# A sixth Strassen pair in the feed-forward blocks of a two-layer trunk

## The reference, cut to what matters

```python
def swiglu(h, w_in, w_out):
    g, u = jnp.split(h @ w_in, 2, axis=-1)
    return (jax.nn.silu(g) * u) @ w_out

for layer in range(DEPTH):          # DEPTH = 2
    ...                             # mixer
    x = x + swiglu(rms_norm(x, ffn_norm[layer]), w_ffn_in[layer], w_ffn_out[layer])
```

## Time and profile before

| | us |
|---|---|
| median of 3 runs | 2021.05 |
| lowest, highest | 2020.53, 2021.08 |
| the profiled execution's own time | 2020.83 |
| its span, first to last instruction | 2019.0 |
| TensorE busy | 2007.1 |
| VectorE busy | 1649.1 |
| ScalarE busy | 1179.2 |

### The profile page before, as it was taken

The page is one execution under the profiler, slowest core; times in us unless marked ns, Lnnn a source line. Parts: engine busy times, 40 slices in busy tenths (PEclk is TensorE's granted clock), DMA queues, the critical chain, the costliest instruction groups (busy, mean ns, idle before and its releaser), DMA issues.

```text
span 2019.0 us, 24662 instructions
## 1 busy us (share of the span) xinstructions
PE 2007.1 (99%) x9266; PEld 1664.0 (82%) x9266; DVE 1649.1 (82%) x1560; ACT 1179.2 (58%) x1195; POOL 170.6 (8%) x216
## 2 busy tenths in 40 slices
PE   9999999999999999999999999999999999999998
PEld 7888888888888888888888887888888888888886
DVE  5666776779999999999987477779999999999995
ACT  6745645555565555665557466565656556655554
POOL 0000000100111110111100000100111101111010
PEclk9999999999999999999999999999999999999999
DMA  8755444857998888998877643766988889888885
GB/s 275 236 188 167 155 150 139 273 195 232 263 270 250 251 242 256 270 260 246 243 236 230 198 138 138 235 223 229 261 256 256 238 254 266 259 259 242 243 261 160
DMA packets 237188, 461.40 MB, mean 229 GB/s; under 512 B 16481, under 2 KB 21377, under 8 KB 236993
## 3 DMA queue, kind: packets, MB, share of 16 engines
q1 hardware_dynamic: 202832, 386.97, 57.0%
q0 software_dynamic: 30496, 69.22, 16.8%
q10 hardware_dynamic: 3792, 4.34, 0.7%
HBM read 401.10 MB, written 17.29 MB: 207 GB/s over the span
## 4 chain that ended last, share of the span: by engine, by line
PE 92%; DVE 5%; ACT 1%; DMA 1%; issue 1%; ACTq 0%; SPq 0%; DVEq 0%
PE ps L1753 58%; PE ps L1538 29%; DVE g_lo L1279 1%; PE ps L1644 1%; DVE w_lo L918 1%; DVE w_lo L1284 1%; DMA raw<-in_w_ab_in 1%; DVE w_sum L1267 0%; PE ps L1564 0%; PE ps L1904 0%; PE ps L1879 0%; ACT junk L509 0%; ACT w_hi L466 0%; PE ps L1892 0%; DMA x<-in_x 0%
## 5 line engine op out<-in xcount | busy, mean ns | idle before, releaser
L1279 DVE TENSOR_TENSOR g_lo<-g_raw,g_hi 128x2048 fp32r<-128x2048 f32 x240 | 547.2, 2287 | 55.6 <-ACT g_hi L718 32.5
L918 DVE TENSOR_TENSOR w_lo<-raw,w_hi 128x1024 fp32r<-128x1024 f32 x248 | 294.6, 1220 | 151.5 <-ACT w_hi L466 144.9
L718 ACT CAST g_hi<-g_raw 128x2048 fp32r<-128x2048 f32 x140 | 265.6, 1912 | 157.7 <-PE ps L1753 151.5
L466 ACT ACTIVATE w_hi<-raw 128x1024 fp32r<-128x1024 f32 x248 | 253.9, 1056 | 144.1 <-DMA raw<-in_w_ab_in 55.4
L711 ACT CAST g_hi<-g_raw 128x2048 fp32r<-128x2048 f32 x100 | 191.5, 1915 | 215.9 <-DVE g_raw L1261 215.9
L1753 PE MATMUL ps<-g_hi,xT_hi 128*128 128x512 f32 x780 | 303.6, 389 | 0.9 <-DVE w_lo L1284 0.8
L1753 PE MATMUL ps<-g_hi,xT_lo 128*128 128x512 f32 x780 | 303.4, 389 | 0.0
L1538 PE MATMUL ps<-w_hi,xT_hi 128*128 128x512 f32 x672 | 264.4, 393 | 0.6 <-DVE w_lo L918 0.6
L1753 PE MATMUL ps<-g_lo,xT_hi 128*128 128x512 f32 x680 | 264.5, 389 | 0.0
L1538 PE MATMUL ps<-w_hi,xT_lo 128*128 128x512 f32 x672 | 261.8, 390 | 0.0
L1538 PE MATMUL ps<-w_lo,xT_hi 128*128 128x512 f32 x672 | 261.6, 389 | 0.0
(11 more groups left out here) (226 smaller groups left out, 3039.8 us busy)
## 6 DMA issues: line engine op xcount, KB each, us to landing
g_raw<-in_w_ffn_in SPq DMA_DIRECT2D x320, 512.0 KB, 4.8
g_raw<-in_w_ffn_out SPq DMA_DIRECT2D x160, 512.0 KB, 4.7
raw<-in_w_ab_in SPq DMA_DIRECT2D x96, 512.0 KB, 4.8
x<-y POOLq DMA_DIRECT2D x80, 512.0 KB, 6.8
raw<-in_w_qkv SPq DMA_DIRECT2D x40, 512.0 KB, 4.6
raw<-in_w_ab_out SPq DMA_DIRECT2D x32, 512.0 KB, 4.9
raw<-in_w_ffn_in SPq DMA_DIRECT2D x32, 512.0 KB, 4.7
raw<-in_w_c_out SPq DMA_DIRECT2D x32, 512.0 KB, 4.7
```

Of the source, the lines that this page charges most:

```text
L466: act.activation(w_hi[:, s, :], raw[:, s % RAWS, :], ACT.Copy).then_inc(hi_ready, 1)
L718: act.copy(dst[:, 0:4, :].rearrange("p s w -> p (s w)"), src[:, :, :].rearrange("p s w -> p (s w)")).then_inc(group_hi_ready, 1)
L918: dve.tensor_tensor(w_lo[:, s, :], raw[:, s % RAWS, :], w_hi[:, s, :], ALU.subtract).then_inc(lo_ready, 1)
L1279: ins = dve.tensor_tensor(lo_part[:, 0:4, :].rearrange("p s w -> p (s w)"), src[:, :, :].rearrange("p s w -> p (s w)"), hi_part[:, 0:4, :] ...
```

## The change

One of the three plain groups becomes a Strassen group: pair 5 now is the sixth "strassen" pair, and the order is S S S P S S S P. The rest of the edits follow from it. The hi places of groups 0 and 3 change roles (`HI_OF`), since group 0 now needs seven tiles. The token sums hold 6 pairs; two of the four `s_lo` move to the place of constants that are no longer read. Inside a Strassen group the three products of x and s_sum 3 that share banks P2, P4, P3 come first, then the four others. In group 0 TensorE waits ahead of P1 and P6 for the third y copy and ahead of P7 and P5 for the fourth; in block 1 it waits at these places for silu and `hidden` of block 0. ScalarE's program has copy 0, hi(0), copy 1, hi(1), copy 2, then the first part of hi(2), copy 3, and the second part of hi(2). Before it was hi(0), copies 0 and 1, hi(1), copy 2, hi(2), copy 3. The two parts of a Strassen hi are the four tiles of the pair and the three sums.

```diff
-GROUPS_UP = [("plain", 5), ("strassen", 0), ("strassen", 1), ("strassen", 2),
-             ("plain", 6), ("strassen", 3), ("strassen", 4), ("plain", 7)]
+GROUPS_UP = [("strassen", 0), ("strassen", 1), ("strassen", 2), ("plain", 6),
+             ("strassen", 3), ("strassen", 4), ("strassen", 5), ("plain", 7)]
+HI_OF = [3, 1, 2, 0]
...
+        s_lo_at = [bias_at + 52 * KB, bias_at + 55 * KB, consts_at + 512, consts_at + 512 + s_size]
...
             def hi_group(f, layer, g, first, base, between=None):
...
                     act.copy(dst[:, 0:4, :].rearrange("p s w -> p (s w)"),
                              src[:, :, :].rearrange("p s w -> p (s w)")).then_inc(group_hi_ready, 1)
+                    if between is not None:
+                        between()
                     act.wait_ge(sum_step, f * (3 * PAIRS) + (layer * BLOCKS * 3 * PAIRS + n + 3))
...
+                    if not first:
+                        copy_y(before, layer, 0)
                     hi_(0)
                     if not first:
-                        copy_y(before, layer, 0)
                         copy_y(before, layer, 1)
                     hi_(1)
                     if not first:
                         copy_y(before, layer, 2)
-                    hi_(2)
-                    if not first:
-                        copy_y(before, layer, 3)
+                    hi_group(f, layer, 2, first, base, None if first else lambda: copy_y(before, layer, 3))
                     hi_(3)
...
-                                      first and q < 2, last and q >= 2)
+                                      first and q == 1 and t == 1, last and q >= 2)
...
-                for bank, a, slot, alone in ((P1, x_part(2 * p, t0), 0, True), (P6, s_part(1), 4, True),
-                                             (P7, s_part(2), 5, True), (P5, s_part(0), 1, True),
-                                             (P2, x_part(2 * p + 1, t0), 2, False), (P4, x_part(2 * p + 1, t1), 6, False),
-                                             (P3, s_part(3), 3, False)):
+                for bank, a, slot, alone in ((P2, x_part(2 * p + 1, t0), 2, False), (P4, x_part(2 * p + 1, t1), 6, False),
+                                             (P3, s_part(3), 3, False),
+                                             (P1, x_part(2 * p, t0), 0, True), (P6, s_part(1), 4, True),
+                                             (P7, s_part(2), 5, True), (P5, s_part(0), 1, True)):
+                    if slot in (0, 5):
+                        shared_free(slot == 5)
...
+                    def shared_free(second):
+                        if first:
+                            pe.wait_ge(silu_ready, 2 * FB * layer + 2)
+                            pe.wait_ge(hid_ready, 2 * FB * layer + 2)
+                        else:
+                            pe.wait_ge(y_copied, f * 4 + (4 * (layer * BLOCKS - 1) + second - 1))
```

More of the change, by code:

```diff
@@ L139, in trunk @@
         u_mid = sb("u_mid", [P, W])
+        consts_at = place[0]
         consts = sb("consts", [P, N_CONST, P])
@@ L197, in trunk @@
         s_hi = [sb(f"s{i}_hi", [P, PAIRS, P], F32R, at=bias_at + 40 * KB + i * s_size) for i in range(4)]
-        s_lo = [sb(f"s{i}_lo", [P, PAIRS, P], F32R, at=bias_at + 50 * KB + i * s_size) for i in range(4)]
+        s_lo_at = [bias_at + 52 * KB, bias_at + 55 * KB, consts_at + 512, consts_at + 512 + s_size]
+        s_lo = [sb(f"s{i}_lo", [P, PAIRS, P], F32R, at=s_lo_at[i]) for i in range(4)]
         s_sum = sb("s_sum", [P, 4, PAIRS, P], at=bias_at + 60 * KB)
@@ L699, in free_group, with hi_group @@
                 if first and g < 4:
-                    act.wait_ge(chunk_used, RING * base + (0, 12, 15, 0)[g])
+                    act.wait_ge(chunk_used, RING * base + (0, 12, 15, 0)[HI_OF[g]])
                 else:
                     act.wait_ge(group_used, f * BLOCK_GROUPS + (group_at(layer, 0) + g - 3))
-            def hi_group(f, layer, g, first, base):
+            def hi_group(f, layer, g, first, base, between=None):
                 free_group(f, layer, g, first, base)
-                src, dst = group_raw[g % 6], group_hi[g % 4]
+                src, dst = group_raw[g % 6], group_hi[HI_OF[g % 4]]
                 if g < N_UP and GROUPS_UP[g][0] == "strassen":
@@ L1766, in plain_group, with strassen_group @@
                         ins = product(bank, xT_hi[:, k, ts], xT_lo[:, k, ts], hi_part[:, q, :], lo_part[:, q, :],
-                                      first and q < 2, last and q >= 2)
+                                      first and q == 1 and t == 1, last and q >= 2)
                 ins.then_inc(group_used, 1)
-            def strassen_group(g, first, last):
-                hi_part, lo_part, sums_lo = group_hi[g % 4], group_lo[g % 6], sum_lo[g % 4]
+            def strassen_group(g, first, last, shared_free):
+                hi_part, lo_part, sums_lo = group_hi[HI_OF[g % 4]], group_lo[g % 6], sum_lo[HI_OF[g % 4]]
                 p = GROUPS_UP[g][1]
@@ L1776, in strassen_group @@
                 s_part = lambda i: (s_hi[i][:, p, :], s_lo[i][:, p, :])
[L1777 to L1780 removed]
+                for bank, a, slot, alone in ((P2, x_part(2 * p + 1, t0), 2, False), (P4, x_part(2 * p + 1, t1), 6, False),
[4 more added lines that the diff above has]
+                        shared_free(slot == 5)
                     w_lo_part = lo_part[:, slot, :] if slot < 4 else sums_lo[:, slot - 4, :]
[L1782 removed]
+                    ins = product(bank, *a, hi_part[:, slot, :], w_lo_part, first, alone and last)
                 ins.then_inc(group_used, 1)
             def down_group(g):
[L1787 removed]
+                hi_part, lo_part = group_hi[HI_OF[g % 4]], group_lo[g % 6]
                 n = g - N_UP
@@ L1802, in block @@
                 def block(f, first, last):
+                    def shared_free(second):
[4 more added lines that the diff above has]
+                            pe.wait_ge(y_copied, f * 4 + (4 * (layer * BLOCKS - 1) + second - 1))
                     for g in range(BLOCK_GROUPS):
+                        if g == 0 and first:
+                            pe.wait_ge(s_ready, 4 * (layer + 1))
                         if g == 0 and not first:
                             pe.wait_ge(out_step, f * 5 + 5 * (layer * BLOCKS - 1))
[L1806 to L1811, removed]
                         if g == N_UP:
@@ L1824, in block @@
                         elif GROUPS_UP[g][0] == "strassen":
-                            strassen_group(g, g == 1, g == LAST_STRASSEN)
+                            strassen_group(g, g == 0, g == LAST_STRASSEN, shared_free if g == 0 else lambda second: None)
                         else:
-                            plain_group(g, g == 0, g == N_UP - 1)
+                            plain_group(g, g == 3, g == N_UP - 1)
                 block(1, True, False)
```

12 lines of the change are left out of this document (6 added, 6 removed).

## The result

The changed kernel takes 2032.24 us (median of 3 runs, 2032.18 to 2032.25), the kernel before 2021.05. The ratio is 1.0057, with a 95% interval of 1.0044 to 1.0071: the sixth pair makes the kernel 11.2 us slower. The prediction was 2034.0, range 2023 to 2046.

A forecast was written before the change was run, and what follows sets the result against it. TensorE was taken to bound the kernel (61.88 us rounds), with VectorE close behind and becoming the bound after the change. Starts 3.5 + 3.9 and rounds 5.9 summed to +13.3 us, giving 2034 us, range 2023 to 2046.

The forecast's parts named there:

- the prediction's own mark: TensorE's start of group 8 in block 1, forecast at 495.7 us in layer 0 and 1412.5 in layer 1.
- the starts: Start of each layer's feed-forward phase: 3.5 us late in layer 0, 3.9 in layer 1, +7.4 together.
- the rounds: Nine steady rounds per layer after block 1: 18 x 0.33 = 5.9 us slower.
- VectorE per round: VectorE's chain in a steady round: +4.47 us against 4.14 to spare, so 62.21 us, 0.33 over the old round.
- TensorE per round: TensorE's matmuls in a steady round: 270 x 0.2268 = 61.24 us, 0.67 less than before.
- a wait before group 6: TensorE in each round waits once ahead of group 6, up to 1 us, for VectorE's w_lo.
- The 0.3 us foreseen at P7: TensorE within group 0 waits some 0.3 us at bank P7 for the fourth y copy.
- VectorE without a wait: Steady round: what VectorE wants from TensorE has over 1 us of slack each, so VectorE never idles.
- The fourth copy fits with nothing to spare: ScalarE, between group 2's hi parts: copy ends at 29.0, second part at 30.5, wanted at 30.55; costed at 0.
- The 1.6 us for the wider token sums: Each layer's start: token sums grow from 5 to 6 pairs, adding 1.6 us to the chain (bounds 0 and 1.6).
- Rival A: Steady round: TensorE stays the bound, VectorE's chain under 61.24 us; 2016.4 us, or 2010 with starts absorbed; chance 0.15.
- Rival B: ScalarE's fourth y copy comes late, 0.5 to 1.3 us a round; +16 us, 2050; chance 0.13.

The follow-up runs named there:

- the run with the short instruction: Changed kernel with VectorE's lo part of the returned hidden rows made for 32 elements instead of 1024 in blocks 2 to 10 (output invalid): 2017.53 us, ratio 0.9987.
- The run with `hidden` first: Changed kernel with `hidden` and `turn_blocks` of block 0 moved ahead of group 2's sums in block 1: 2033.07 us, ratio 1.0065.
- the first five-pair run: Changed kernel with pair 5 plain again and token sums five pairs wide, new order and moved copies kept: 2024.49 us, ratio 1.0022.

## Why the prediction was right, and by how much each step was off

The mechanism held: VectorE's chain ends the round and the start. The sum, +13.3 against +11.2 measured (11.4 in the spans), is closer than its parts. By group 8, the prediction's own mark, the starts cost 8.35 where it had 7.4, and the rounds 3.05 where it had 5.9. The two errors have opposite signs, and that part of the closeness is luck.

Two lines of the kernel before, of VectorE's and of ScalarE's timeline, that the first step below goes back to:

```profile
1724.34 1.31 DVE L1208 STREAM_TRANSPOSE hid_blk<-hid 128x512 f32<-128x512 f32 x2
...
1723.76 1.91 ACT L718 CAST g_hi<-g_raw 128x2048 fp32r<-128x2048 f32 x1 [2.36 <-PE ps L1753]
```

- *VectorE per round, 62.21 predicted, +0.33.* Measured 62.14 in layer 0 and 62.07 in layer 1, +0.26 and +0.19. This is the most mis-sized term. I took VectorE's spare time as the sum of its listed idle times, 4.14. There was a fifth that isn't listed. `turn_blocks` began at 1724.34 and the lo part of group 0 at 1725.70, 1.36 us later, just behind ScalarE's hi copy (1723.76 + 1.91 = 1725.67). Now a sum that needs no copy follows, after 1.23 us (1673.55 to 1674.78). That is 0.13 us. Another 0.06 lies between u_mid and `turn_blocks` (10.85 us before, 10.79 after), which makes 4.33 to spare. Against it stands what the pair costs. Group 0 takes 6.64 us from 1674.78 to 1681.42, where the plain group took 2.21. And the plain lo part of group 3 starts 1.75 us after w_lo (1693.10 to 1694.85), 0.08 more than between the others: it starts as ScalarE's copy of group 3 ends, which is queued behind the fourth y copy (1692.91 + 1.91 = 1694.82). 4.43 + 0.08 - 4.33 = 0.18, which is this round (62.06). The 0.07 more of layer 0 was not traced.
- *TensorE per round, 61.24, with a wait before group 6.* 61.20 in the run with the short instruction: the piece of 583.74 us counts its last matmul at full length, and 61.88 / 273 is 0.2267. The wait is 0.53 us listed; from start to start it is 0.91 (1717.44 to 1718.35) against 0.227, 0.68 us. The 0.3 us foreseen at P7 are not seen.
- *VectorE without a wait, over 99% busy.* No idle is listed, but the union of its instructions is 60.69 of 62.06 us, 98%: the small gaps between dependent instructions are in both kernels and aren't spare.
- *The fourth copy fits with nothing to spare.* It began 27.9 us behind u_mid (28.1 predicted). The second hi part of group 2 was in time; hi(3), queued behind it, which the prediction left out, was late by the 0.08 us above. The run with the copy one place later pays for the same queue.
- *The starts, 3.5 + 3.9.* Measured by group 8: 3.24 + 5.11. In layer 0 the first sum of block 1 began at 439.09 (439.7 predicted), and u_mid followed after 52.31 us (52.4 predicted). In layer 1 it began at 1361.34 (1355.0 + 1.6 + 5.28 = 1361.9 with the loss of layer 0) and took 53.07, of which 0.68 is the wait in front of u_mid. Group 8 then came 4.62 us behind u_mid in place of 3.6. These last two no step of mine had: TensorE is late there (last section). 0.64 us of it comes back in the next round, which takes TensorE 61.43 us in place of 62.07. The 1.6 us for the wider token sums are there: in layer 1 the first weights are asked for 1.62 us later (1356.57 against 1349.67 + 5.28). But they landed after 4.75 us where it was 5.24.
- *Rival A* needed VectorE's chain below 61.24 us: 0.8 us away; the short instruction, which took 1.0 us off, made it true, and its 2017.5 us are near the 2016.4 that the prediction had for it. The 6.67 us that spoke against A stand in the trace of before as said, though twice and twice (groups 2 and 3, 5 and 6), with plain work between, not four times running. *Rival B* is what happens without the moved copies; with them the adds landed after 6.9 us in the median, 6.8 before.

## What to carry to other kernels

When two engines are within a few per cent of each other, work a trade between them out per round on the waiting engine's own chain: spare time before, less what is added, against the saving of the other. Here 3 matmuls (0.67 us) were bought for 4.5 us of VectorE with 4.3 to spare. Listed idle times are a lower bound of what is spare; compare start-to-start distances where an instruction of another kind will follow. And when an edit lengthens an engine's chain, ask for each small instruction on the engines beside it what is queued behind it: the fourth 1 us copy was all but free in one place and cost 4 us of kernel one place later, and the first one cost 42 us more when it stood behind a copy that waits for VectorE.

## What the hardware showed unasked

TensorE's clock fell after some waits. Windows of the kernel after (length, busy time and instructions of each engine, then the granted TensorE clock, 1.00 being 2.4 GHz and 0.50 1.2 GHz), behind the waits of 3.14 us (layer 0) and 3.89 us (layer 1):

```profile
456.50:459.60 3.10, 3.06 (x7) 2.48 (x8) 3.10 (x3) 1.88 (x2) 0.56 (x1) 0.50 0.17 67
...
1378.80:1384.60 5.80, 5.80 (x14) 4.54 (x15) 5.80 (x5) 1.83 (x2) 1.69 (x3) 0.50 0.22 90
```

At 0.50 the matmuls follow each other after 0.43 us instead of 0.227. The 7 of layer 0 leave no wait in front of u_mid, since VectorE is the later one. The 14 of layer 1 cost TensorE 14 x 0.2 = 2.8 us, and in the chain of waits it is TensorE that runs from there through u_mid:

```profile
1378.80 40.41 PE ps L1757 x165
```

165 matmuls at 0.2268 would be 37.4 us; 3.0 more are lost. TensorE being 3 us late is enough to explain why VectorE waits 0.68 us for `gu` ahead of u_mid at 1414.41, which it doesn't at 491.40. The run with `hidden` first shows the same in another place: after its wait for hid (1.49 us in layer 1) the clock stays up, after the wait of 2.73 us ahead of group 6 it falls for some 8 matmuls, and VectorE again waits in front of u_mid, 0.79 us. In layer 0 of that run the wait of 2.73 us, and in the first five-pair run one of 2.76 us, were followed by no slow matmul. The windows behind the two waits of 2.73 us, layer 0 and layer 1:

```profile
486.00:489.50 3.50, 3.50 (x17) 2.90 (x16) 3.50 (x2) 2.36 (x2) 0.00 (x0) 1.00 0.40 152
...
1409.40:1412.60 3.20, 3.20 (x9) 2.52 (x8) 3.20 (x3) 1.48 (x1) 0.00 (x0) 0.50 0.17 64
```

So the length of the wait alone doesn't decide, and what else does was not tested. In VectorE's chain it is worth about 0.7 us here, in one of two layers. It also means that the stall at the start is not quite free in layer 1, as I had read it first: it is free beside VectorE's chain, and the clock behind it is not.
